# One encoder kernel: values kept in token layout, and the rows of maxima moved by a transfer

## The chip, the core and the metric

The kernel runs on one core of a Trainium2 chip. The core has five engines with instruction streams of their own: TensorE (PE, matmuls), VectorE (DVE), ScalarE (ACT), GpSimd (POOL) and SyncE (SP), which in this kernel issues the transfers (DMAs). They meet at semaphores. The metric is the time of one execution in device microseconds. For the kernel before it is 3714.93 us, the median of three runs (3707.92, 3714.93, 3715.57).

## The reference

Two layers of an encoder run over 1280 tokens of 1024 features: one sequence of 1024 tokens and one of 256, with shared weights. What matters here is the mixer of each layer:

```
h = RMSNorm(x); z = h @ w_in
A: latent attention, 4 heads (keys and values from a low-rank latent, rotary part beside them)
B: dilated windows (128,1), (512,4), (2048,16) joined by their softmax denominators, bias by distance, 4 heads
C: grouped queries, 8 heads on 2 key/value heads, per-head norm of q and k, 2-D rotary
p = softmax(scale * q k^T + bias);  o = p v
x = x + RMSNorm(concat(A, B, C) @ w_out)
x = x + RMSNorm(ConvGatedMLP(RMSNorm(x)))
```

The result is float32 throughout, and the kernel keeps that accuracy on TensorE by splitting each operand into a high and a low part: a product is high x high, low x high and high x low, so three matmuls.

## The kernel before

Each layer runs through phases with a barrier of all engines between them: `latent_projections`, `head_projections`, `attention`, output projection and normalisation, then the gated MLP. The change touches the first three.

**Projections.** Activations lie with features on the partitions and tokens along the row. A projection unit makes 128 features of all 1280 tokens: weights are the stationary operand and tokens the moving one, in blocks of 512, 512 and 256, three matmuls for each of eight chunks of 128 input features (helper `product`, L224 to L226). A unit ends in three banks of PSUM, ACT copies it to a stage buffer in one instruction of 1280 columns (L1034), and SP stores it to a DRAM tensor `heads`, one row per feature (L892). The weights of the next units come in by transfers from SP (L636), ACT rounds them to the high part (L645), and POOL subtracts to get the low part (L650). The phase has twelve units, five of which are roped (norm and rotary) on DVE and POOL; the last three (`VB`, `VC`, `VB+P`) are values. The values of group A come from two units of the latent phase.

**Attention.** Sixteen heads follow each other without a gap (A: 0 to 3, B: 4 to 7, C: 8 to 15). A head is 18 steps, held in the table `STEPS`: query blocks of 512, 512 and 256 columns against tiles of 128 keys. The three blocks begin at steps 0, 4 and 9. On PE, step i is: `scores` (L1288; three matmuls in A, four in B, two in C), then the *side work* that the function `side_work` gives for the step, then `values` of step i-3 (L1300, L1301, L1303). ACT takes the exponential twice (L1412, L1413), DVE subtracts to get the low part of the probabilities, which this text calls `p_low` (L1578). Scores of step i wait for `p_low` of step i-3.

The softmax is shifted by the row's maximum. Maxima of a head come ahead of its steps: 18 matmuls (L1319, in B a bias matmul L1322 behind each) make blocks of q k^T, and DVE reduces them (L1532, L1535, L1542) to columns of the tile `m`, which hold one number per query on 128 partitions. The shift is added inside the scores' matmul, through one extra row of the q operand: partition 96 of `q1` in A, partition 64 of `q2` in B and C. So the columns have to become a row. This is done in three pieces (`ROW_TILES`: 4, 2 and 4 tiles of 128 queries, for the blocks that begin at steps 0, 4 and 9). `turn_row` transposes a strip of 65 columns per tile (L1340) so that the row of interest lands on partition 0 of one PSUM bank with the tiles side by side, and `copy_row` on ACT writes 1 x 512 or 1 x 256 numbers into the q operand's row (L1393). Pieces 0 and 1 are side work of steps 15 and 17 of the head before, piece 2 of step 7 of the head itself. The first scores of a block wait for its piece (`row_copied`).

Nine heads of each layer bring new keys and values (1 to 8 and 12; head 0's are made ready in the phase ahead). Their values lie in DRAM with features on rows, are loaded as 64 x 1280 (`vt`, L1247), turned tile by tile on PE as side work of steps 3 (eight transposes) and 11 (two), both L1330, and split by DVE out of PSUM (L1551, L1553).

**Queues.** The order of each engine is written out by hand; nothing reorders it. SP's order in attention is: q of head h, k of head h, for B two bias lines (`graw`, L1245), values of head h, each behind waits for the buffers that they fill.

## Time and profile before

| | |
|---|---|
| median of three runs | 3714.93 us (3707.92 to 3715.57) |
| the profiled execution's own time | 3715.99 us |
| its span, first to last instruction | 3714.2 us |
| PE busy in the span | 3633.3 us (98%), 18267 matmuls |
| DVE, ACT, POOL busy | 1847.0 (50%), 1552.6 (42%), 1148.6 us (31%) |
| mean granted clock of PE | 0.991 |
| attention, first and second layer (from the span's start) | 325.7 to 799.5 and 2158.0 to 2634.5 us |

How to read it: "busy" is the time in which an engine has an instruction in work. Matmuls overlap, so the duration of one (0.39 us for 512 columns) is longer than what it adds to the engine's time; what it adds is read from the starts of two that follow each other. A matmul row of the profile names out<-in by the program's tiles, `ps` being PSUM. In brackets stands the idle time ahead of an instruction and what ended it.

### The profile page before, as it was taken

Reading aid. Unit: us, or ns where it says so; the run is one execution under the profiler, and the core shown is the slowest. Engines: PE = TensorE matmul, PEld = TensorE weight load, DVE = VectorE, ACT = ScalarE, POOL = GpSimd, SP = SyncE. Lnnn points to the kernel's source line nnn. Section 1 sums busy time; section 2 is a strip of 40 time slices with the busy share of each in tenths; the row PEclk is TensorE's granted clock in tenths of the full one; section 3 lists DMA queues with packets and bytes.
Section 4 is the critical chain, followed back from the end, with each engine's and each line's share of the span. In section 5 each row is a group of like instructions: output and inputs, shape, how many; then the busy total and the mean of one; then the engine's idle time right before and its main releaser. Section 6 shows DMA issues by size and latency. Waiting matters only on the chain. (4 is left out here: it accounts for less than half of the span.)

```text
span 3714.2 us, 49843 instructions
## 1 busy us (share of the span) xinstructions
PE 3633.3 (98%) x18267; PEld 3003.9 (81%) x18267; DVE 1847.0 (50%) x2900; ACT 1552.6 (42%) x2515; POOL 1148.6 (31%) x835
## 2 busy tenths in 40 slices
PE   8999999999999999999999999999999999999998
PEld 7787777778788888888767877777788888888886
DVE  4135868955433333344551367689463333344335
ACT  4334878974222121221442367789542122211213
POOL 1134443443321221221342334434343221221213
PEclk9999999999999999999999999999999999999999
DMA  5342321022111111111324323111221111111113
GB/s 173 124 111 68 75 68 33 22 80 91 46 40 40 40 40 34 40 40 34 113 67 143 97 68 86 47 40 32 71 95 46 40 40 34 40 40 34 35 45 113
DMA packets 205965, 234.00 MB, mean 63 GB/s; under 512 B 15968, under 2 KB 164486, under 8 KB 205767
## 3 DMA queue, kind: packets, MB, share of 16 engines
q1 hardware_dynamic: 205807, 231.93, 21.4%
q8 instruction: 94, 1.54, 0.2%
q14 instruction: 64, 0.52, 0.0%
HBM read 173.86 MB, written 51.48 MB: 61 GB/s over the span
## 5 line engine op out<-in xcount | busy, mean ns | idle before, releaser
L224 PE MATMUL ps<-hh,wh 128*128 128x512 f32 (+1 forms) x2688 | 969.0, 360 | 16.4 <-PEq L218 12.6
L225 PE MATMUL ps<-hl,wh 128*128 128x512 f32 (+1 forms) x2688 | 955.8, 356 | 0.0
L226 PE MATMUL ps<-hh,wl 128*128 128x512 f32 (+1 forms) x2688 | 954.5, 355 | 0.0
L2495 POOL TENSOR_TENSOR wl<-raw,wh 128x1024 fp32r<-128x1024 f32 x126 | 301.7, 2401 | 1269.1 <-ACT wh L2328 1269.1
L224 PEld LDWEIGHTS ps<-hh,wh 128*128 128x128 f32 x2688 | 510.4, 190 | 95.1 <-issue 19.0
L2556 DVE SCALAR_TENSOR_TENSOR cb<-ps,params,cb 128x1023 f32<-128x1023 f32 (+1 forms) x172 | 143.9, 878 | 871.5 <-ACT cb L2337 871.5
L225 PEld LDWEIGHTS ps<-hl,wh 128*128 128x128 f32 x2688 | 510.6, 190 | 76.6 <-issue 5.7
L226 PEld LDWEIGHTS ps<-hh,wl 128*128 128x128 f32 x2688 | 510.1, 190 | 72.1
L1578 DVE TENSOR_TENSOR pl<-ps,ph 128x512 fp32r<-128x512 f32 (+1 forms) x576 | 375.6, 653 | 53.8 <-ACT ps L1413 53.4
L1532 DVE TENSOR_REDUCE mx<-ps 128x1 f32<-128x512 f32 x480 | 330.9, 689 | 142.0 <-PE ps L1322 82.8
L1412 ACT ACTIVATE ph<-ps 128x512 fp32r<-128x512 f32 (+1 forms) x576 | 330.0, 573 | 162.2 <-PE ps L1288 157.1
L1288 PE MATMUL ps<-q,k 97*128 97x512 f32 (+4 forms) x1296 | 384.9, 388 | 8.1 <-PEq L218 6.2
L2337 ACT ACTIVATE cb<-ps,params 128x1280 f32<-128x1280 f32 x86 | 122.3, 1422 | 645.0 <-PE ps L226 635.2
L2587 DVE TENSOR_TENSOR y<-ps,y 128x512 f32<-128x512 f32 (+1 forms) x480 | 279.7, 600 | 179.0 <-PE ps L226 176.4
L224 PE MATMUL ps<-ah,wh 128*128 128x512 f32 (+1 forms) x960 | 341.3, 356 | 0.0
L225 PE MATMUL ps<-al,wh 128*128 128x512 f32 (+1 forms) x960 | 341.3, 356 | 0.0
L226 PE MATMUL ps<-ah,wl 128*128 128x512 f32 (+1 forms) x960 | 339.6, 354 | 0.0
L1413 ACT ACTIVATE ps<-ps 128x512 f32<-128x512 f32 (+1 forms) x576 | 328.6, 571 | 0.0
L2328 ACT ACTIVATE wh<-raw 128x1024 fp32r<-128x1024 f32 x126 | 130.4, 1050 | 431.3 <-PE ps L226 422.3
L1288 PEld LDWEIGHTS ps<-q,k 97*128 97x128 f32 (+2 forms) x1296 | 238.2, 190 | 67.4 <-DVE pl L1578 11.8
L1300 PE MATMUL ps<-ph,vh 128*128 128x512 f32 (+1 forms) x576 | 231.6, 402 | 0.0
L1303 PE MATMUL ps<-pl,vh 128*128 128x512 f32 (+1 forms) x576 | 219.9, 382 | 0.0
(271 smaller groups left out, 5633.7 us busy)
## 6 DMA issues: line engine op xcount, KB each, us to landing
raw<-in_w_up SPq DMA_DIRECT2D x88, 512.0 KB, 3.9
heads<-stage SPq DMA_DIRECT2D x38, 640.0 KB, 3.1
raw<-in_w_down SPq DMA_DIRECT2D x44, 512.0 KB, 3.7
rq<-heads SPq DMA_DIRECT2D x56, 320.0 KB, 4.8
raw<-in_w_in SPq DMA_DIRECT2D x32, 512.0 KB, 4.3
rk<-heads SPq DMA_DIRECT2D x32, 320.0 KB, 4.7
raw<-in_w_out SPq DMA_DIRECT2D x16, 512.0 KB, 4.4
residual<-my SPq DMA_DIRECT2D x32, 256.0 KB, 2.0
```

Of the source, the lines that this page charges most:

```text
L224: pe.matmul(out, wh, xh, start=(k == 0), stop=False)
L225: pe.matmul(out, wh, xl, start=False, stop=False)
L226: last = pe.matmul(out, wl, xh, start=False, stop=(k == len(pairs) - 1))
L1288: mm = pe.matmul(out, a, b, start=(k == 0), stop=(k == len(prods) - 1))
L1300: pe.matmul(out, c.vh[kv(h)][:, kt, :], c.ph[g % RING][:, 0:w], start=first, stop=False)
L1303: pe.matmul(out, c.vh[kv(h)][:, kt, :], c.pl[g % RING][:, 0:w], start=False, stop=last).then_inc(pv_done, 1)
L1412: act.activation(c.ph[g % RING][:, 0:w], scores, ACT.Exp, scale=STEP_SCALE[kind(h)]).then_inc(exp_done, 1)
L1413: act.activation(scores, scores, ACT.Exp, scale=STEP_SCALE[kind(h)]).then_inc(exp_done, 1)
L1532: dve.tensor_reduce(c.mx[:, qt, kb:kb + 1], bank(c, b, w), AX.X, ALU.max).then_inc(max_taken, 1)
L1578: dve.tensor_tensor(c.pl[g % RING][:, 0:w], bank(c, ST + g % 3, w), c.ph[g % RING][:, 0:w].bitcast(F32), ALU.subtract).then_inc(p_low, 1)
L2495: pool.tensor_tensor(c.wl[slot][:], c.raw[parity][:], c.wh[slot][:].bitcast(F32), ALU.subtract).then_inc(w_lo, units)
L2587: dve.tensor_tensor(c.y[:, o, t0:t0 + w], bank(c, DOWN_BANKS[u], w), c.y[:, o, t0:t0 + w], ALU.add).then_inc(down_added, 1)
```

## The change

Values are now computed in token layout. In the head phase the normalised activations are the stationary operand (128 tokens at a time) and the value weights the moving one: ten tiles of 128 tokens, each with eight chunks of three matmuls over 384 columns (all of B's and C's values). In the latent phase five groups of two tiles make A's values, 256 columns each. They are stored to a new DRAM tensor `values`, one row per token. The value weights get buffers of their own, whose low part lies where the buffers of the rotary work lay, so POOL's split of them waits until the fifth unit is roped. In attention, values come in as 128 x 10 x 64 and are split by DVE from that buffer (SBUF), in one piece of 640 columns behind `p_low` of step 9; the transposes on PE are gone.

Each piece of the row of maxima is now one transpose, of 4 or 2 columns of `m` into 4 or 2 partitions of 128. ACT copies those to a small buffer `row_part`, and a transfer from SP moves them into the q operand's row. The first scores of a block wait for the transfer (`row_landed`) instead of the copy. Piece 2 is turned at step 6 in A and head 8, 7 in B, 5 in heads 9 to 15. On SP, pieces 0 and 1 of head h-2 stand ahead of the q loads of head h, and piece 2 behind the k loads and ahead of the bias lines.

```diff
+def value_columns(c, col):
+    return c.s_v[:, col:col + 64].rearrange("(t p) n -> p t n", p=P)
+def split_head_values(dve, c, slot, n):
+    dve.tensor_copy(c.vh[slot][:, :, 0:64], c.vt[:]).then_inc(c.v_hi, 1)
+    dve.wait_ge(c.v_hi, n + 1)
+    dve.tensor_tensor(c.vl[slot][:, :, 0:64], c.vt[:], c.vh[slot][:, :, 0:64].bitcast(F32), ALU.subtract).then_inc(c.v_lo, 1)
...
-    UNITS = 12
+    UNITS = 9
+    LOADS = 12
...
+                pe.wait_ge(w_lo, LOADS - 2)
+                for t in range(NT):
+                    pe.wait_ge(evacuated, UNITS - 1 if t < 3 else UNITS if t < 6 else UNITS + t - 5)
+                    ts = slice(t * P, t * P + P)
+                    product(pe, bank(c, VALUE_BANKS[t % 6], V_COLS),
+                            [(c.hh[:, k, ts], c.hl[:, k, ts], c.wv_hi[:, k, :], c.wv_lo[k // 5][:, k % 5, :]) for k in range(KC)],
+                            lambda k: side(KC * t + k)).then_inc(w_used, 1)
...
+                            pool.wait_ge(w_hi, UNITS + u - 1)
+                            pool.wait_ge(roped, len(ROPED))
+                            pool.tensor_tensor(c.wv_lo[0][:, :, cols], raw[:, 0:5, :], c.wv_hi[:, 0:5, cols].bitcast(F32), ALU.subtract)
...
+    OUT_SPLITS = ((HEADS - 2, 11), (HEADS - 2, 16), (HEADS - 1, 7), (HEADS - 1, 12))
...
+    def third_row(h):
+        return 19 - max_lead(h)
...
-        if i in (3, 11) and h >= 0 and new_kv(h + 1):
-            work.append(("values", h + 1, (i - 3) // 8))
-        if i == 7 and 0 < h < HEADS:
+        if 0 < h < HEADS and i == third_row(h):
             work.append(("row", h, 2))
...
+                def move_row(h, r):
+                    t0, t1 = ROW_TILES[r]
+                    sp.wait_ge(row_copied, 3 * h + r + 1)
+                    row = c.q1[h % 3][96:97, :] if kind(h) == "A" else c.q2[h % 3][64:65, :]
+                    sp.dma_start(row[:, t0 * P:t1 * P].bitcast(F32).rearrange("a (k p) -> a k p", p=P),
+                                 c.row_part[r][0:t1 - t0, :].bitcast(F32)).then_inc(row_landed[r], 16)
...
-                    if first:
-                        pe.wait_ge(row_copied, 3 * h + block + 1)
+                    if first and h == 0:
+                        pe.wait_ge(row_copied, block + 1)
+                    elif first:
+                        pe.wait_ge(row_landed[block], 16 * h)
...
-                    for k, qt in enumerate(range(*ROW_TILES[r])):
-                        m0 = max_column(qt)
-                        mm = pe.transpose(bank(c, b, P, slice(0, ROW_WINDOW), off=k * P), c.m[:, m0:m0 + ROW_WINDOW], c.ident[:])
-                    mm.then_inc(row_turned, 1)
+                    m0 = max_column(ROW_TILES[r][0])
+                    pe.transpose(bank(c, b, P, slice(0, row_tiles(r))), c.m[:, m0:m0 + row_tiles(r)], c.ident[:]).then_inc(row_turned, 1)
...
-                    t0, t1 = (x * P for x in ROW_TILES[r])
-                    row = c.q1[h % 3][96:97, t0:t1] if kind(h) == "A" else c.q2[h % 3][64:65, t0:t1]
-                    act.activation(row, bank(c, b, t1 - t0, slice(0, 1)), ACT.Copy).then_inc(row_copied, 1)
+                    if h >= 2:
+                        act.wait_ge(row_landed[r], 16 * (h - 1))
+                    rows = slice(0, row_tiles(r))
+                    act.activation(c.row_part[r][rows, :], bank(c, b, P, rows), ACT.Copy).then_inc(row_copied, 1)
...
+                    if i == 9 and new_kv(h + 1):
+                        split_values(h + 1)
```

Where the work stands on the engines, before and after, is shown at three places. (The numbers behind a name tell buffers of one name apart.)

On PE, head 1, step 3: between the side matmul of a maximum and the values of an earlier step stand the eight transposes of head 2's values.

```order
L1319 MATMUL ps<-k_1_114,q_1_108 128x512
L1330 MATMUL ps<-ident,vt 128x64 x8
L1300 MATMUL ps<-ph_131,vh_123 128x512
L1301 MATMUL ps<-ph_131,vl_125 66x512
L1303 MATMUL ps<-pl_135,vh_123 128x512
```

In the changed kernel the values (now L1396) follow the maximum (now L1415) at once.

```order
L1415 MATMUL ps<-k_1_114,q_1_108 128x512
L1396 MATMUL ps<-ph_132,vh_123 128x512
L1397 MATMUL ps<-ph_132,vl_125 66x512
L1399 MATMUL ps<-pl_136,vh_123 128x512
L1384 MATMUL ps<-q_1_108,k_1_114 128x256
```

On PE, head 5 (kind B), steps 7 to 9: piece 2 of the row is turned, and two groups of values and the scores of step 8 later the first scores that need it begin.

```order
L1340 MATMUL ps<-ident,m 65x128 x4
L1300 MATMUL ps<-ph_131,vh_123 128x256
L1301 MATMUL ps<-ph_131,vl_125 66x256
L1303 MATMUL ps<-pl_135,vh_123 128x256
L1288 MATMUL ps<-q_2_116,k_1_114 128x512
L1288 MATMUL ps<-q_2_119,k_1_115 128x512
L1288 MATMUL ps<-gh_189,flip_r 128x512
L1288 MATMUL ps<-gl_191,flip_r 128x512
L1319 MATMUL ps<-k_0_120,q_0_117 128x512
L1322 MATMUL ps<-gh_188,ident_r 128x512
L1300 MATMUL ps<-ph_132,vh_123 128x512
L1301 MATMUL ps<-ph_132,vl_125 66x512
```

In the changed kernel one transpose (L1427) stands in the place of four, with the same work behind it.

```order
L1427 MATMUL ps<-ident,m 4x128
L1396 MATMUL ps<-ph_132,vh_123 128x256
L1397 MATMUL ps<-ph_132,vl_125 66x256
L1399 MATMUL ps<-pl_136,vh_123 128x256
L1384 MATMUL ps<-q_2_116,k_1_114 128x512
L1384 MATMUL ps<-q_2_119,k_1_115 128x512
L1384 MATMUL ps<-gh_196,flip_r 128x512
L1384 MATMUL ps<-gl_198,flip_r 128x512
L1415 MATMUL ps<-k_0_120,q_0_117 128x512
L1418 MATMUL ps<-gh_195,ident_r 128x512
L1396 MATMUL ps<-ph_133,vh_123 128x512
L1397 MATMUL ps<-ph_133,vl_125 66x512
```

On SP in attention, the transfers for head 4: its q and k (`rq`, `rk`), its bias lines and its values.

```order
L1224 DMA rq<-heads 64x1280 x2
L1238 DMA rk<-heads 64x1280 x2
L1245 DMA graw_186<-distance_lines 128x960
L1245 DMA graw_187<-distance_lines 128x960
L1247 DMA vt<-heads 64x1280
```

In the changed kernel head 2's three pieces of the row (L1284) stand among them, two ahead of the q loads and the third between the k loads and the bias lines.

```order
L1284 DMA q_2_116<-row_part_126 1x4x128
L1284 DMA q_2_116<-row_part_140 1x2x128
L1302 DMA rq<-heads 64x1280 x2
L1318 DMA rk<-heads 64x1280 x2
L1284 DMA q_2_116<-row_part_141 1x4x128
L1327 DMA graw_193<-distance_lines 128x960
L1327 DMA graw_194<-distance_lines 128x960
L1329 DMA vt<-values 128x10x64
```

## Rows read from the trace of the kernel before

**Rows 1.** Busy time in the two attention stretches: their sum, then each engine.
```profile
sum 950.30, PE 947.02 PEld 736.14 DVE 772.90 ACT 782.95 POOL 430.80; mean PE 473.51 PEld 368.07 DVE 386.45 ACT 391.48 POOL 215.40
```

**Rows 2.** Timeline of PE, head 1 step 3 (start us, duration us, engine, line, instruction).
```profile
359.76 0.40 PE L1319 MATMUL ps<-k,q 96*128 96x512 f32 x1
360.09 0.71 PE L1330 MATMUL ps<-ident,vt 64*128 64x64 f32 x8
...
361.06 0.40 PE L1301 MATMUL ps<-ph,vl 128*66 128x512 f32 x1
```

**Rows 3.** Timeline of PE, head 0 step 11, the pair of transposes.
```profile
343.58 0.33 PE L1330 MATMUL ps<-ident,vt 64*128 64x64 f32 x2
...
344.19 0.39 PE L1301 MATMUL ps<-ph,vl 128*66 128x512 f32 x1
```

**Rows 4.** Timeline of PE, end of a C head into the next.
```profile
745.91 0.39 PE L1319 MATMUL ps<-k,q 128*128 128x512 f32 x1
746.14 0.60 PE L1340 MATMUL ps<-ident,m 128*65 128x128 f32 x4
...
746.81 0.39 PE L1301 MATMUL ps<-ph,vl 128*66 128x512 f32 x1
...
747.97 0.28 PE L1300 MATMUL ps<-ph,vh 128*128 128x256 f32 x1
748.09 0.28 PE L1301 MATMUL ps<-ph,vl 128*66 128x256 f32 x1
...
749.03 0.38 PE L1340 MATMUL ps<-ident,m 128*65 128x128 f32 x2
...
749.48 0.40 PE L1301 MATMUL ps<-ph,vl 128*66 128x512 f32 x1
...
749.95 0.63 PE L1288 MATMUL ps<-q,k 128*128 128x512 f32 x2
```

**Rows 5.** Timeline of ACT in the same stretch.
```profile
747.48 0.59 ACT L1393 ACTIVATE q<-ps 1x512 fp32r<-1x512 f32 x1
```

**Rows 6.** Timeline of ACT, head 5 step 7.
```profile
503.84 0.58 ACT L1393 ACTIVATE q<-ps 1x512 fp32r<-1x512 f32 x1
```

**Rows 7.** Timeline of PE, head 5 step 9, first scores.
```profile
505.85 0.63 PE L1288 MATMUL ps<-q,k 128*128 128x512 f32 x2
```

**Rows 8.** DMA issues: out<-in, queue, count, KB each, median us to landing.
```profile
raw<-in_w_in SPq DMA_DIRECT2D x32, 512.0 KB, 4.3
residual<-my SPq DMA_DIRECT2D x32, 256.0 KB, 2.0
...
rot<-stage SPq DMA_DIRECT2D x80, 80.0 KB, 2.6
```

**Rows 9.** Timeline of PE, the first matmuls of attention.
```profile
325.70 2.00 PE L1288 MATMUL ps<-q,k 97*128 97x512 f32 x5 [3.21 <-PEq L218]
```

**Rows 10.** Timeline of DVE, head 1 steps 9 to 11.
```profile
373.03 0.68 DVE L1578 TENSOR_TENSOR pl<-ps,ph 128x512 fp32r<-128x512 f32 x1
...
374.66 0.28 DVE L1551 CAST vh<-ps 128x128 fp32r<-128x128 f32 x1
...
375.18 0.68 DVE L1578 TENSOR_TENSOR pl<-ps,ph 128x512 fp32r<-128x512 f32 x1
```

**Rows 11.** Timeline of PE, head 1 step 13, its scores.
```profile
376.63 0.52 PE L1288 MATMUL ps<-q,k 97*128 97x256 f32 x3
```

**Rows 12.** Timeline of DVE in the head phase, the fifth roped unit.
```profile
260.89 1.49 DVE L1101 TENSOR_TENSOR rot<-rot,st 128x1280 f32<-128x1280 f32 x1
263.43 2.91 DVE L1104 TENSOR_TENSOR stage<-rot,pr 128x1280 f32<-128x1280 f32 x1 [1.05 <-ACT pr L1000]
```

**Rows 13.** Timeline of POOL in the same stretch.
```profile
262.59 2.40 POOL L650 TENSOR_TENSOR wl<-raw,wh 128x1024 fp32r<-128x1024 f32 x1 [8.19 <-ACT wh L645]
```

**Rows 14.** Timeline of ACT in the head phase, units 7 and 8.
```profile
261.47 1.05 ACT L645 ACTIVATE wh<-raw 128x1024 fp32r<-128x1024 f32 x1
...
274.54 1.24 ACT L1034 ACTIVATE stage<-ps 128x1280 f32<-128x1280 f32 x1 [11.21 <-PE ps L226]
```

More of the change, by code:

```diff
@@ L171, in place_buffers @@
     c.vl = [take(f"vl{i}", [P, NT, VL_COLS], F32R) for i in range(2)]
+    vl_end = at[0]
+    c.row_part = [take("row_part0", [P, P], F32R)]
     at[0] = max(at[0], projections_end)
@@ L698, in _ @@
                 sp.dma_start(c.s_z[QAR:QAR + P, :], c.stage[1][:]).then_inc(stored[1], 16)
-                for j in range(2, 8):
+                for j in range(2, 6):
                     sp.wait_ge(evacuated, 3 + j)
@@ L755, in _ @@
                             aux(9 + b, [(c.perm_a[:], c.stage[1][:, t0:t0 + w])], slice(0, P), w)
+                for g in range(5):
+                    pe.wait_ge(evacuated, 7 if g < 3 else 8)
+                    for i in range(2):
+                        ts = slice(256 * g + P * i, 256 * g + P * i + P)
+                        last = product(pe, bank(c, VALUE_BANKS[g], 256, off=256 * i),
+                                       [(c.lath[:, 2, ts], c.latl[:, 2, ts], c.kv_hi[:, 256:512], c.kv_lo[:, 256:512])])
+                    last.then_inc(unit_done, 1)
             @block.scalar
@@ L791, in _ @@
                 act.activation(c.lath[:, 2, :], c.lat[2][:], ACT.Copy).then_inc(lat_hi, 1)
-                for j in range(1, 8):
+                for j in range(1, 6):
                     m = 3 + j
@@ L801, in _ @@
                         act.activation(c.wh[i][:], c.raw[i][:], ACT.Copy).then_inc(head_hi, 1)
+                for g in range(5):
+                    act.wait_ge(unit_done, 6 + g)
+                    act.activation(value_stage(g), bank(c, VALUE_BANKS[g]), ACT.Copy).then_inc(evacuated, 1)
             @block.gpsimd
@@ L889, in store, with store_values @@
                         sp.wait_ge(evacuated, n + 1)
-                    done = stored[n % 3] if n < UNITS - 3 else c.heads_stored
-                    sp.dma_start(c.s_z[rows[n]:rows[n] + P, :], c.stage[n % 3][:]).then_inc(done, 16)
+                    sp.dma_start(c.s_z[rows[n]:rows[n] + P, :], c.stage[n % 3][:]).then_inc(stored[n % 3], 16)
+                def store_values(tiles):
+                    for t in tiles:
+                        sp.wait_ge(evacuated, UNITS + t + 1)
+                        sp.dma_start(c.s_v[t * P:t * P + P, VB:VB + V_COLS], value_stage(t)).then_inc(c.heads_stored, 16)
                 def turn(n):
@@ L901, in turn @@
                         sp.dma_start(c.rot[n % 2][g:g + 16, :], c.stage[n % 3][from_row:from_row + 16, :]).then_inc(turned[n % 2], 16)
[L903 removed]
+                for n in range(2, LOADS):
                     if n - 4 in ROPED:
@@ L912, in _ @@
                 sp.dma_start(c.rq[64:96, :], c.s_z[QAR + 32:QAR + 64, :]).then_inc(c.q_raw, 16)
-                for n in range(UNITS - 4, UNITS - 2):
-                    store(n)
+                store(UNITS - 1)
                 sp.wait_ge(c.k_lo, 3)
@@ L1017, in _ @@
                         roots(n - 1, (0, 1))
-                    if n == TURN_ROWS:
-                        for r in range(3):
-                            first_row(r)
                     act.wait_ge(w_used, n + 1)
@@ L1107, in _ @@
                     first_maximum(j)
-                for part in range(2):
-                    first_values(part)
+                dve.wait_ge(head0, 16 * 5)
+                split_head_values(dve, c, 0, 0)
         end_phase(nc, raw_arrived + [w_hi, w_lo, w_used, tables, evacuated, squared, unit_sum, sum_read, turn_read,
@@ L1204, in side_read @@
                 return max_taken, NM * h + j + 1
-            if what == "values":
-                return v_lo, 2 * (kv_count(h) - 1) + j + 1
             return row_copied, 3 * h + j + 1
@@ L1215, in _ @@
                         continue
+                    if h >= 3:
+                        for r in range(2):
+                            move_row(h - 2, r)
                     sp.wait_ge(q_hi, 3 * h)
@@ L1253, in _ @@
                     sp.dma_start(c.raw[n % 2][:], out_unit(c, L, n)).then_inc(weights[n % 2], 16)
+                for r in range(3):
+                    move_row(HEADS - 2, r)
+                sp.wait_ge(scored, NS * 14)
+                for n in range(2):
+                    load_out_weights(n)
+                for r in range(2):
+                    move_row(HEADS - 1, r)
+                for n in range(2, 4):
+                    load_out_weights(n)
+                move_row(HEADS - 1, 2)
+                for n in range(4, OUT_EARLY + 2):
+                    load_out_weights(n)
                 for i in range(2):
@@ L1323, in max_scores @@
                     mm.then_inc(max_scored, 1)
-                def turn_values(h, part, b):
-                    if h >= 1:
-                        pe.wait_ge(v_raw, 16 * (kv_count(h) - 1))
-                    for t in (range(8) if part == 0 else range(8, 10)):
-                        mm = pe.transpose(bank(c, b, 64, off=(t % 8) * 64), c.vt[0:64, t * P:t * P + P], c.ident[0:64, 0:64])
-                    mm.then_inc(v_turned, 1)
                 def turn_row(h, r, b):
@@ L1352, in _ @@
                             max_scores(h, j, side_bank[item])
-                        elif what == "values":
-                            turn_values(h, j, side_bank[item])
                         else:
@@ L1570, in _ @@
                             take_max(head, j, side_bank[what, head, j])
-                        elif what == "values":
-                            split_values(head, j, side_bank[what, head, j])
                     if 0 <= g < G_TOTAL:
@@ L2737, in encoder @@
     c.s_z = nc.dram_tensor("heads", (Z_ROWS, T), F32, kind="Internal").ap()
+    c.s_v = nc.dram_tensor("values", (T, Z_COLS), F32, kind="Internal").ap()
     c.s_line = nc.dram_tensor("distance_lines", (H_B, N_DIST), F32, kind="Internal").ap()
```

163 lines of the change are left out of this document (93 added, 70 removed).

## The prediction

> **What bounds the kernel now.** I read the busy times of the whole span first: TensorE is busy 98% of it, every other engine half or less. Then the two attention stretches by windows: PE 947.0 of 950.3 us [rows 1], so 3.3 us of idle time lies in them, and whatever leaves PE's order there shortens the kernel by what it adds to that order, unless a new wait takes its place. Last I read the timelines around each kind of instruction that the change touches, and always the starts: a matmul of 512 columns adds 0.235 us to PE's time (two lie between 749.48 and 749.95), one of 256 columns 0.12 (747.97 to 748.09) [rows 4].
>
> **What goes.** Transposes of values. Head 1's eight: the maximum ahead starts at 359.76, the second values matmul behind at 361.06 [rows 2]. Without the transposes these two would lie 2 x 0.235 apart, so the eight cost 1.30 - 0.47 = 0.83 us. From the first transpose to that matmul it is 0.97 [rows 2], with two transposes 0.61 (343.58 to 344.19) [rows 3]: six fewer save 0.36, so two cost 0.47. Nine heads in two layers: 18 x (0.83 + 0.47) = 23.4 us. Head 0's values are turned in the same way in the head phase, also on PE: 2 x 1.30 = 2.6.
>
> Transposes of the rows. Four take 0.90 (745.91 to 746.81) minus 0.47 = 0.43; two take 0.22 less (746.14 to 746.81 against 749.03 to 749.48: 0.67 and 0.45) [rows 4], so 0.21. One is then about 0.11. Fifteen heads, two layers: 60 of four and 30 of two become 90 single ones: 25.8 + 6.3 - 9.9 = 22.2. If a single transpose cost as much as a pair, it would be 13.2.
>
> Evacuation at the end of two phases. The last copy of 1280 columns takes 1.24 (274.54) [rows 14], 512 take 0.59 [rows 5], so a column adds 0.85 ns, 384 take 0.48, a latent group's 512 take 0.59. PE waits for the store and the barrier behind that copy, 3.21 us ahead of attention [rows 9]. Two layers: 2 x (0.76 + 0.65) = 2.8.
>
> **What is added on PE.** The value products have the columns of before (per layer 240 x 384 = 3 units x 24 x 1280 in the head phase, 30 x 256 = 2 x 3 x 1280 in the latent one), but 36 more matmuls. A cut adds 2 x 0.12 - 0.235, at most 0.01 [rows 4]: 72 x 0.013 = 0.9 us at most, which I take.
>
> **The value weights' wait.** POOL may split them only when the fifth roped unit is done. DVE's last step of it starts at 263.43 and takes 2.91 beside POOL's split of a unit's weights, which ends at 264.99 [rows 12, 13]. In the changed kernel that split is what waits, so the step may take the 1.49 of its neighbour [rows 12] and end at 264.92, or 266.34 as now. Then for the third set: POOL's split of the first set frees its buffer (2.40) [rows 13], the load lands 4.3 later [rows 8], ACT rounds it (1.05) [rows 14], POOL splits it (2.40): 10.2 us with nothing for the hand-overs, 275.1 or 276.5. PE is done with unit 8 shortly ahead of 274.54 [rows 14], say 274.4: it waits 0.7 to 2.1 us. I take the middle with a little for hand-overs, 1.6, twice: 3.2. The nearest cover is the matmuls of that unit itself; a load that lands at twice 4.3 would make it 6 each.
>
> **Rows that come by a transfer.** This is the largest unknown: no row shows a transfer of 2 KB between partitions of SBUF. The nearest rows are the 128 x 512 store (2.0 us to landing) and the stage-to-rot moves inside SBUF, which go in trains of eight (2.6) [rows 8]; a load of 512 KB takes 4.3 [rows 8]. I take 1.95, with 1.7 and 3.5 as ends. To it comes ACT's copy (0.59 - 384 x 0.85 ns = 0.26) [rows 5, 14] and some 0.03 to the issue, a guess. The time that is there is read from before as the start of ACT's copy to the first scores of the block, less the PE time that the transposes gave up between them. Piece 0 in C: 747.48 to 749.95 = 2.47 [rows 4, 5], less 0.32 for its own turn (ACT's copy follows exponentials of scores ahead of the turn, so it stays where it is while the first scores come sooner) and 0.1 for piece 1's: 2.05. Piece 2 in B: 503.84 to 505.85 = 2.01 [rows 6, 7], less 0.32 = 1.69; head 7's follows with three matmuls less and has about 1.2. By the same reading piece 0 of A has 2.7, piece 2 of A (now one step earlier) 2.6, of head 8 2.4, of C (two steps earlier) 3.5, and piece 1 over 5 anywhere. Needed are 0.29 + 1.95 = 2.24: C's piece 0 waits 0.19 (heads 9 to 15, two layers: 14 x 0.19 = 2.7), B's piece 2 0.55 (6 x = 3.3), head 7's 1.04 (2 x = 2.1): 8.1 us. At 1.7 it is 3.4, at 2.6 some 26, at 3.5 some 67, since then A's pieces wait too. On SP piece 2 stands behind k loads, which wait for POOL's split of the keys before, work of steps 0 to 2 of that head, so they are out ahead of the turn. Behind the pieces stand the bias lines, which the next head but one uses, and the q loads, which may now leave only after step 17 of head h-3, but which POOL needs from step 9 of head h-2. So I cost the queue at nothing; if a load's wait ran past the turn, piece 2 would land later by as much.
>
> **The split by DVE.** It is one block of two instructions on 640 columns, where before 512 columns were split at step 3 and 128 at step 11. A two-operand instruction between SBUF tiles of 1280 columns takes 1.49 [rows 12], so I take 0.8 for each half, 1.6 in all. In A: `p_low` of step 9 starts at 373.03, gives DVE free at 373.65, the split runs to 375.25, the maximum (0.61 as the step between starts) to 375.86, `p_low` of step 10 to 376.54; scores of step 13 start at 376.63 [rows 10, 11]. It just fits, because the two small instructions that go (374.66 to 375.18, 0.52) [rows 10] stood in the same gap. The next `p_low` is then some 0.3 late: 8 x 0.3. In B a step has more matmuls and it fits. Head 11's steps are the shortest (two matmuls of scores): about 1 us late, twice. Sum 2.4 + 2 = 4.4. It is 0 if the halves take half of that, and 18 x (1.49 + 0.1) at most if each waits out another engine as the row of 2.91 did: 29.
>
> On that row: DVE's step is held 1.4 us while POOL reads SBUF [rows 12, 13]. The Trainium skill ("SBUF — State Buffer", Who interferes with whom) says why: DVE and GpSimd share one pair of ports by an exclusive lock, and a DVE instruction with two SBUF inputs, or a copy in a two-port mode, fully blocks against GpSimd. The trace agrees (2.91 against 1.49). It speaks against the change, since values were split out of PSUM before and are now split from SBUF; it is the second rival below. The skill's "VectorE: DVE Perf Modes" (Mode 2×_2P) would make the rounding copy twice as fast between SBUF buffers. No row here shows such a copy; by that rule the sum would be some 3 us lower.
>
> **Sum.** Gone: 23.4 + 2.6 + 22.2 + 2.8 = 51.0. Added: 0.9 + 3.2 + 8.1 + 4.4 = 16.6. 3715.99 - 34.4 = 3681.6 for an execution like the profiled one; the median lies 1.1 below that one's own time, so 3680.5, and I write 3681.
>
> **Rivals.** (1) The new waits are covered: the landing is 1.7 or less and DVE and the weights make nobody wait. Then 47 to 50 go: 3665 to 3668, 3666. For it: a piece is 2 KB, and the 2.0 is that of 256 KB. Against it: B's piece 2 has 1.69 us, which asks for a landing of 1.4.
> (2) DVE's split is held by POOL. POOL splits q of the head after next at its steps 9, 11 and 13, around DVE's step 9. If each split takes 3.0 instead of 1.6 (the 1.4 of the held row on top), the excess by the same chain of starts is 1.7 in A (0.9 in head 3), 0.4 to 1.2 in B, 2.3 in head 11, together 21 instead of 4.4: 3697. Against it: POOL is busy 430.8 of 950.3 us [rows 1], so a split meets it less than half the time.
> (3) The pieces land late, which makes it slower. Place: the first scores of blocks 0 and 2, 60 of 90 pieces. From a landing of 2.6 on, a further 0.9 costs 41 us, so 46 per us; the gain of 34.4 on top of 8.1 is used up at 2.6 + (42.5 - 26) / 46 = 2.96 us. At 3.5 the time is 3681 + 59 = 3740. For it: 512-byte pieces and a destination of one partition, and loads that share the queue. Against it: the moves inside SBUF take 2.6 though they leave eight at a time [rows 8].
> (4) A single transpose has a fixed cost and takes what a pair does: 9 us less gain, 3690. The step from four to two (0.22) speaks for proportion.
>
> **Chances and range.** The forecast 0.58; (1) 0.14; (2) 0.12; (3) 0.10; (4) 0.06. The likeliest case alone, with landings of 1.7 to 2.2 and DVE's term between 0 and 9, spans 3672 to 3692. The range holds (1), (2), (4) and landings to 2.6 (3681 + 18 = 3699); with DVE held and a landing of 2.4 (18 instead of 8.1) it is 3707, where it ends. Its low end stands 4 under (1): PE's waits for DVE's split out of PSUM, behind the values transposes, go too, and the sum leaves them out. About 0.2% (7.4 us) is what a measurement of this kernel can tell from no change. Faster by more: 0.58 + 0.14 + 0.06 and most of (2), 0.87. Within it: 0.05, the part of (3) near 2.9 and worst sums of (2). Slower: 0.08.
>
> **What would show it.** PE's row turns are single matmuls that push the next start by 0.11; PE's busy time in the two attention stretches falls by some 45 us. Waits of scores that begin a block show who is late: on a DMA from `row_part` in C's block 0 and B's block 2, by 0.2 and 0.55, or not. The transfers' median landing decides between (1), the forecast and (3). The rows of the split on DVE show 0.8 and 0.8, or one of 1.5 and more with POOL beside it. In the head phase PE stands idle 1 to 2 us ahead of the first value product. The forecast is wrong if the landing is over 2.2, if the scores of steps 13 and 14 wait for DVE by more than 0.5 in A, or if PE waits where nothing of this is.

## The result and the profile after

The changed kernel takes 3677.25 us (median of four runs, 3675.38 to 3678.59); the kernel before, beside it, 3715.25 (3707.92 to 3717.63). The ratio is 0.9901 with an interval of 0.9889 to 0.9912, so 37 us less, where 34 were forecast (3681). The span of the profiled execution falls from 3714.2 to 3676.4.

The first lines of the page after the change: the span, then busy time, share of the span and number of instructions of each engine.

```profile
span 3676.4 us, 49277 instructions
...
PE 3588.7 (98%) x17929; PEld 2974.7 (81%) x17929; DVE 1833.9 (50%) x2860; ACT 1525.4 (41%) x2535; POOL 1151.8 (31%) x841
```

TensorE's share is still 98%, so the kernel became shorter by what left PE's order, less what turned into waiting. To see how much that is, both traces are cut at the same events: from attention's first scores to its last. First the kernel before, then the changed one (window, its length, busy us of each engine, granted clock as a share of full speed, share of the DMA engines, GB/s).

```profile
325.70:796.65 470.95, 469.26 (x2227) 364.94 (x2228) 384.60 (x670) 389.25 (x758) 214.66 (x234) 1.00 0.21 51
2158.04:2631.55 473.51, 471.96 (x2227) 366.88 (x2228) 384.62 (x670) 389.32 (x758) 214.65 (x234) 0.99 0.20 51
sum 944.46, PE 941.22 PEld 731.82 DVE 769.22 ACT 778.57 POOL 429.30; mean PE 470.61 PEld 365.91 DVE 384.61 ACT 389.28 POOL 214.65
```

```profile
326.56:779.84 453.28, 447.92 (x2032) 344.36 (x2033) 379.76 (x652) 374.39 (x758) 215.74 (x234) 1.00 0.21 53
2140.44:2595.30 454.86, 449.13 (x2033) 345.60 (x2034) 380.96 (x652) 374.56 (x758) 215.87 (x234) 1.00 0.21 53
sum 908.14, PE 897.06 PEld 689.96 DVE 760.72 ACT 748.95 POOL 431.61; mean PE 448.53 PEld 344.98 DVE 380.36 ACT 374.48 POOL 215.81
```

PE is busy 44.2 us less (45 was forecast), the stretches are 36.3 shorter; PE's idle time in them rises from 3.2 to 11.1. Some 2.6 us of the 36.3 are not the change but the clock that PE was granted in the execution before (the account of the prediction ends with it). The remaining 1.5 us of the span went in the other phases. What PE waits for in the first layer's stretch now (us in total, times, longest):

```profile
PE ps L1384 <- DVE pl L1656: 2.9, 7, 0.8
PE ps L1384 <- PEq L235: 2.2, 1, 2.2
PE ps L1415 <- ACT gh L1471: 1.1, 1, 1.1
PE ps L1384 <- DMA q<-row_part: 0.6, 1, 0.6
```

The second row is the barrier ahead of attention (its start stands for [rows 9]). The other three are for DVE's split (before, 0.9 us in four waits for `p_low` stood here) and for a row piece, which the forecast had, and for ACT's `gh`, which it had not. This view counts only idle time, and a wait comes out larger when it is read from the starts of the matmuls; the amounts below are from starts.

The row piece of head 4, block 2. (Head 5, which [rows 6] and [rows 7] show before, waits by the same 0.29.) PE, with the single transpose at 458.90:

```profile
458.67 0.39 PE L1418 MATMUL ps<-gh,ident_r 128*128 128x512 f32 x1
458.90 0.27 PE L1427 MATMUL ps<-ident,m 128*4 128x128 f32 x1
458.92 0.36 PE L1396 MATMUL ps<-ph,vh 128*128 128x256 f32 x1
459.13 0.28 PE L1397 MATMUL ps<-ph,vl 128*66 128x256 f32 x1
...
461.21 0.39 PE L1399 MATMUL ps<-pl,vh 128*128 128x512 f32 x1
461.74 0.47 PE L1384 MATMUL ps<-q,k 128*128 128x512 f32 x1
```

ACT's copy, and SP's issue of the transfer with the first bias line behind it:

```profile
459.65 0.25 ACT L1478 ACTIVATE row_part<-ps 4x128 fp32r<-4x128 f32 x1
```

```profile
459.92 0.65 SPq L1284 DMA_DIRECT2D q<-row_part  x1
460.62 0.44 SPq L1327 DMA_DIRECT2D graw<-distance_lines  x1
```

From 458.67 to 459.13 are 0.46; less 0.235 and 0.12 for the two matmuls, the transpose adds 0.11. From issue to the scores that wait are 461.74 - 459.92 = 1.82 us. The scores would have begun at 461.21 + 0.235 = 461.45, so the wait is 0.29. The packet records of the trace divide the 1.82: the piece's four packets lie between 461.21 and 461.30, so 1.29 us pass from the issue to the first packet, 0.09 in the packets and 0.44 from the last one to the scores. Of all 90 pieces the first packet begins 1.22 to 1.34 us behind the issue.

DVE's split, head 0 in the second layer, with POOL and PE beside it (`CAST vh<-vt` and the subtraction behind it stand where [rows 10] has `CAST vh<-ps`):

```profile
2156.18 0.68 DVE L1656 TENSOR_TENSOR pl<-ps,ph 128x512 fp32r<-128x512 f32 x1
2156.78 0.93 DVE L619 CAST vh<-vt 128x640 fp32r<-128x640 f32 x1
2157.74 1.79 DVE L621 TENSOR_TENSOR vl<-vt,vh 128x640 fp32r<-128x640 f32 x1
2159.46 0.68 DVE L1617 TENSOR_REDUCE mx<-ps 128x1 f32<-128x512 f32 x1
```

```profile
2156.75 0.61 POOL L1527 CAST q<-rq 96x512 fp32r<-96x512 f32 x1
2157.44 1.41 POOL L1534 TENSOR_TENSOR q<-rq,q 96x512 fp32r<-96x512 f32 x1
```

```profile
2160.79 0.39 PE L1384 MATMUL ps<-q,k 97*128 97x256 f32 x1 [1.30 <-DVE pl L1656]
```

This is the dearest of the 18 splits in attention: 2.7 us, and the scores of step 13 wait. Over all 20 of the kernel the second half takes 825 ns at least and 826 in the median; the smallest, the median and the largest stand here in ns:

```profile
L621 DVE TENSOR_TENSOR vl<-vt,vh x20: 825/826/1795, 304.2 to 2491.9; 128x640 fp32r<-128x640 f32 x20
```

### The profile page after: what moved, and what is told of

It is laid out like the page before. It is cut to its first block and busy times, and to the rows that moved or that the text cites. A ratio compares the mean times of both kernels' runs of the same rounds, so it can differ in the third digit from the quotient of the medians.

```text
span 3676.4 us, 49277 instructions
## 1 busy us (share of the span) xinstructions
PE 3588.7 (98%) x17929; PEld 2974.7 (81%) x17929; DVE 1833.9 (50%) x2860; ACT 1525.4 (41%) x2535; POOL 1151.8 (31%) x841
## 3 DMA queue, kind: packets, MB, share of 16 engines
q8 instruction: 91, 1.49, 0.2%
## 5 line engine op out<-in xcount | busy, mean ns | idle before, releaser
L241 PE MATMUL ps<-hh,wh 128*128 128x512 f32 (+1 forms) x2544 | 917.0, 360 | 18.2 <-PEq L235 14.3
L242 PE MATMUL ps<-hl,wh 128*128 128x512 f32 (+1 forms) x2544 | 904.1, 355 | 0.0
L243 PE MATMUL ps<-hh,wl 128*128 128x512 f32 (+1 forms) x2544 | 903.1, 355 | 0.0
L241 PEld LDWEIGHTS ps<-hh,wh 128*128 128x128 f32 x2544 | 483.3, 190 | 92.7 <-issue 20.8
L242 PEld LDWEIGHTS ps<-hl,wh 128*128 128x128 f32 x2544 | 483.4, 190 | 72.4 <-issue 5.7
L243 PEld LDWEIGHTS ps<-hh,wl 128*128 128x128 f32 x2544 | 482.7, 190 | 68.1
L1396 PE MATMUL ps<-ph,vh 128*128 128x512 f32 (+1 forms) x576 | 226.8, 394 | 0.0
```

Source lines behind the costliest of these rows:

```text
L241: pe.matmul(out, wh, xh, start=(k == 0), stop=False)
L242: pe.matmul(out, wh, xl, start=False, stop=False)
L243: last = pe.matmul(out, wl, xh, start=False, stop=(k == len(pairs) - 1))
L1396: pe.matmul(out, c.vh[kv(h)][:, kt, :], c.ph[g % RING][:, 0:w], start=first, stop=False)
```

## The experiments

Each was timed in five rounds beside the kernel before. The intervals are some 5 to 6 us to either side, so a term of 3 us is read from the traces, and the times only have to agree.

**One part alone.** `values_only` takes the values in token layout and leaves four transposes per row; `rows_only` moves the rows by a transfer and leaves the values. Of `side_work`, against the changed kernel, the first:

```diff
-        if 0 < h < HEADS and i == third_row(h):
+        if i == 7 and 0 < h < HEADS:
```

and the second:

```diff
+        if i in (3, 11) and h >= 0 and new_kv(h + 1):
+            work.append(("values", h + 1, (i - 3) // 8))
```

> The kernel before with the token-layout values alone: products, stores, loads and DVE's split as changed, the rows of maxima as before (four or two transposes, ACT's copy, piece 2 at step 7). By the prediction's terms: 23.4 + 2.6 + 2.8 less 0.9, 3.2 and 4.4, so 20.3 us faster than before (ratio 0.9945). Rival: DVE's split from SBUF and the new value weights give back most of what the transposes gave, then under 8 us faster (over 0.998). If the two parts are independent, this gain and that of the rows alone add up to the 38 us of the whole; if both end at the same engine in some heads (ACT in head 3, DVE in C), their sum is larger by 3 us or more.

> The kernel before with the moved rows alone (one transpose per piece, ACT's copy of 4 partitions, transfer, piece 2 at step 6, 7 or 5), values as before. By the prediction's terms 22.2 less 8.1, so 14 us faster (0.996); by the waits that the changed kernel's trace shows on row_part (3.2 instead of 8.1) 19 us (0.995). Rival: the transfers land in time only because the values' transposes are gone, and here SP's or DMA's queue makes them late: then over 8 us of waits on row_part and a gain under 14.

Measured: values alone 0.9945 (0.9931 to 0.9958), 20 us less; rows alone 0.9948 (0.9934 to 0.9962), 19 less. Together 40, the whole change 37 with intervals of about 5 on each: within these the parts add. In the traces they do so in most heads. Head 1, from its first scores to the next head's, takes 30.33 before, 29.23 with values alone, 29.63 with rows alone, 28.50 with both (1.10 + 0.70 against 1.83). Head 7 takes 35.56, 34.25, 35.66 and 34.33: there the rows alone cost 0.10, since piece 2 comes late. Head 3 gets only 0.28 from values alone (33.93 to 33.65), and its trace says why: the wait for ACT stands there already without the rows.

```profile
421.98 0.47 PE L1377 MATMUL ps<-k,q 128*128 128x512 f32 x1 [1.24 <-ACT gh L1435]
```

**The landing.** `b_row6` turns piece 2 of B heads a step earlier; `bias_first` lets the bias lines go ahead of it.

```diff
-        return 19 - max_lead(h)
+        return 18 - max_lead(h) if 4 <= h < 8 else 19 - max_lead(h)
```

```diff
-                    if h >= 3:
-                        move_row(h - 2, 2)
                     if kind(h) == "B":
...
                             sp.dma_start(c.graw[i][:], src).then_inc(table_raw, 16)
+                    if h >= 3:
+                        move_row(h - 2, 2)
                     sp.wait_ge(v_lo, n)
```

> The changed kernel with piece 2 of the B heads turned at step 6 instead of 7 (as A has it). The changed kernel waits 0.29 us for it in heads 4 to 6 and 0.72 in head 7, in both layers 3.2 us, and with one step (2 us) more all of that goes, unless the last maximum of a B head (step 5) isn't reduced when PE comes to the turn: by DVE's rows that takes some 0.9 us of the 2.1 of a step, so PE shouldn't wait. 3 us less than the changed kernel, some 40 under before. Rival: the piece is late because SP or the queue is, not because its turn is; then the wait on row_part stays at 0.29 and 0.72.

> The changed kernel with piece 2 of head h-2 behind the bias lines of head h on SP instead of ahead of them (heads 4 to 7). By the prediction the place costs nothing unless a load's wait runs past the turn: the lines of heads 5 to 7 wait for POOL's low part of the table before (issued at steps 7.5, 6.8 and 6.8 of heads 3 to 5 in the kernel before), so piece 2 of head 3 lands about 1 to 1.5 us later and its scores at step 9 wait by some 1 us; heads 2, 4 and 5 wait by 0 to 0.7 more: 1.5 to 5 us slower than the changed kernel over both layers. Rival: the lines ahead cost nothing, or bring a gain, since the table of head 4 comes sooner.

`b_row6` came as expected: 0.988 (0.9865 to 0.9895), 3673.45; all waits for rows are gone and no other came. Heads 4 to 7 are 4.0 us shorter over both layers. `bias_first` missed by far: 0.9943 (0.993 to 0.9957), 3694.47, 17 us over the changed kernel. SP and PE in head 2:

```profile
389.08 1.06 SPq L1325 DMA_DIRECT2D graw<-distance_lines  x2
391.49 0.66 SPq L1284 DMA_DIRECT2D q<-row_part  x1
```

```profile
396.66 0.70 PE L1384 MATMUL ps<-q,k 97*128 97x512 f32 x2 [2.54 <-DMA q<-row_part]
```

The issue is not late here (ACT's copy, at 391.21, sets it; in head 3 alone it comes 1.3 us behind the copy), but from issue to scores it takes 5.17 us, in heads 3 to 5 3.81, 3.03 and 2.94. The rows' waits sum to 17.9 us over both layers instead of 3.2.

**Is it the queue?** I took it that a piece waits behind the lines in SP's own queue. `row2_act` gives it another: ACT issues piece 2 of heads 2 to 5 right behind its copy.

```diff
-                    if h >= 3:
+                    if h >= 3 and kind(h) != "B":
                         move_row(h - 2, 2)
...
                     act.activation(c.row_part[r][rows, :], bank(c, b, P, rows), ACT.Copy).then_inc(row_copied, 1)
+                    if r == 2 and 2 <= h <= 5:
+                        act.wait_ge(row_copied, 3 * h + r + 1)
...
+                        act.dma_start(row[:, 4 * P:8 * P].bitcast(F32).rearrange("a (k p) -> a k p", p=P),
+                                      c.row_part[2][0:4, :].bitcast(F32)).then_inc(row_landed[2], 16)
```

> The changed kernel with piece 2 of heads 2 to 5 issued by ACT right behind its copy, from ACT's own queue, so that SP issues the bias lines at once as in the kernel before, ahead of the piece in time. With the lines ahead on SP's queue the piece of head 2 took 5.17 us from its issue to the scores, against 1.81 where nothing stands ahead. If a transfer waits for those issued earlier on its own queue, the piece on ACT's queue lands as fast as ever: waits of at most 0.3 us in heads 4 and 5 and none in 2 and 3, the time of the changed kernel or 1 us more for ACT's issues. Rival: the lines keep the 16 engines busy whoever issues; then the scores of heads 2 and 3 wait over 1.5 us as they did with the lines first, and the time is some 10 us over the changed kernel.

Measured: 0.9938 (0.9924 to 0.9951), 3689.97, 13 over the changed kernel: the theory of the queue falls. Head 3: ACT's issue, SP's lines, the scores, and the stretch between (the last two numbers but one are PE's granted clock and the DMA engines' share):

```profile
426.81 0.61 ACTq L1482 DMA_DIRECT2D q<-row_part  x1
```

```profile
427.01 0.80 SPq L1327 DMA_DIRECT2D graw<-distance_lines  x2
```

```profile
430.86 0.47 PE L1384 MATMUL ps<-q,k 97*128 97x512 f32 x1 [1.18 <-DMA q<-row_part]
```

```profile
426.81:430.86 4.05, 2.87 (x14) 2.03 (x13) 2.65 (x5) 2.12 (x4) 3.53 (x5) 1.00 0.50 185
```

The piece is issued 0.20 us ahead of the lines, on another queue, and takes 4.05 us all the same, with the 16 DMA engines half busy. In the changed kernel's head 4 the same stretch is 1.82 long and the engines are idle:

```profile
459.92:461.74 1.82, 1.68 (x9) 1.02 (x7) 1.25 (x3) 1.09 (x2) 1.52 (x3) 1.00 0.00 1
```

So what delays a small transfer is a large one in work beside it, whichever queue it came by. The packet records show where: in head 3 the lines' packets run from 428.34 on, and the piece's own four, 0.2 us long together, come only at 430.02, 3.21 behind the issue. Nor is ACT's queue slow by itself. In heads 4 and 5, where the lines' packets begin 0.9 to 1.0 us ahead of the issue in both kernels, the piece's first packet comes 2.0 to 2.3 us behind the issue on SP's queue (`bias_first`) and 2.1 to 2.2 on ACT's. What the piece waits for ahead of its first packet, no run shows. What the order on SP buys is 0.7 us of start ahead of the lines (459.92 against 460.62), and that was enough. The Trainium skill ("DMA: Bandwidth & Descriptors", Issuing engines are not separate DMA queues) says that the queues of the issuing engines share the same 16 DMA engines; the 4.05 agrees with it.

**The split by DVE.** `split12` does it at step 12; `poolq12` leaves it and moves POOL's split of q from steps 9, 11, 13 to 12, 14, 16.

```diff
-                    if i == 9 and new_kv(h + 1):
+                    if i == 12 and new_kv(h + 1):
```

```diff
-                    if i in (9, 11, 13) and h + 2 < HEADS:
+                    if i in (12, 14, 16) and h + 2 < HEADS:
...
```

> The changed kernel with DVE's split of the values behind p_low of step 12 instead of 9. Step 13 is a block of 256 columns, so its p_low is short and its scores come with more slack. If the lost time is the split's place in DVE's chain, PE's waits for p_low at steps 13 and 14 in heads 0, 1, 2 and 11 (5.3 us over both layers) fall to under 1.5, and the kernel is some 4 us faster than the changed one: about 41 under before. Rival: the split holds PE wherever it stands, then the waits move to steps 16 and 17 with the same sum and the time stays.

> The changed kernel with POOL's split of q at steps 12, 14 and 16 instead of 9, 11 and 13; DVE's split stays at step 9. If POOL's reads of SBUF hold DVE's split, all 18 splits in attention take 0.48 and 0.83 us (in the changed kernel up to 0.94 and 1.79 in heads 0, 2 and 3), PE's waits at steps 13 and 14 of heads 0 and 2 fall to the 0.13 of head 1 (together some 2.5 us less), and head 11's 1.0 stays. Rival: the long ones have another cause (the load of the next values, ACT), then they stay.

`split12`: 0.9891 (0.9876 to 0.9906), 3672.14. Every split takes 0.48 and 0.83, and the waits of the scores of steps 13 and 14 are gone; in their place maxima wait by 0.20 in head 1 and 0.50 in head 11, where a row's turn waits by 0.36 too.

```profile
L621 DVE TENSOR_TENSOR vl<-vt,vh x20: 825/826/828, 302.2 to 2486.2; 128x640 fp32r<-128x640 f32 x20
```

`poolq12`: 0.9895 (0.988 to 0.991), 3673.74. In head 2 POOL no longer stands beside, the split is short and the wait falls from 0.50 to 0.13; head 11 keeps 0.84 and 0.91 of its 1.00 and 0.98: its steps are too short for 1.3 us, with POOL beside or not.

```profile
396.65 0.48 DVE L619 CAST vh<-vt 128x640 fp32r<-128x640 f32 x1
397.17 0.83 DVE L621 TENSOR_TENSOR vl<-vt,vh 128x640 fp32r<-128x640 f32 x1
```

Head 0 was not helped: its split still meets POOL (0.91 and 1.79 in the first layer), since POOL's instructions there follow their loads and not the steps. Where POOL is beside it the split is long, where it is not it is short, in three kernels: that settles what holds it. The Trainium skill ("SBUF — State Buffer", Who interferes with whom) says that the two engines share a pair of SBUF ports by a lock, and that the one that comes second waits for the whole instruction of the first; the long rows agree.

**ACT's table.** In head 3 ACT rounds B's bias table at steps 3 and 4. `table_early` does that at steps 13 and 15 of head 2.

```diff
+                    if i in (13, 15) and h == 2:
+                        split_table(4, (i - 13) // 2)
-                    if i in (3, 4) and kind(h + 1) == "B":
+                    if i in (3, 4) and h >= 4 and kind(h + 1) == "B":
```

> The changed kernel with ACT's rounding of head 4's bias table (two of 0.99 us) moved from steps 3 and 4 of head 3 to steps 13 and 15 of head 2. The changed kernel waits 1.28 us at step 6 of head 3 for the second of them, in each layer. If ACT's own order in the first steps of head 3 is the cause (six roundings of k, two of the table, and the exponentials), that wait goes and so does part of head 3's 0.67 at step 4: 2.6 to 4 us less than the changed kernel. Rival: the bias lines come late, since they stand behind piece 2 on SP; then ACT waits for them in head 2 and PE loses there what it gains in head 3.

0.9889 (0.9874 to 0.9905), 3674.22. The wait for `gh` is gone from both layers; a wait of 0.67 at step 4 of head 3 stays, and one layer has a new one of 0.8 in head 3's first steps.

**The stores of the latent values.** `stores3` sends the five stores of 256 tokens as three.

```diff
-                for g in range(5):
+                for g, n in ((0, 2), (2, 2), (4, 1)):
...
```

> The changed kernel with A's values stored from the latent phase in three transfers (512, 512 and 256 tokens) instead of five. PE stands idle 3.5 and 3.7 us behind that phase in the changed kernel, 2.7 and 3.1 before, though ACT's last copy is shorter. If SP's issues are what the barrier waits for (0.77 us each, the last three from 135.00 to 137.30), two fewer take 1 to 1.5 us off each gap: 2 to 3 us in all. Rival: the landing of the last store or its rows of 1 KB set it; then the gaps stay.

0.9886 (0.987 to 0.9901), 3672.76. PE's gap between the two projection phases, by starts, falls from 3.76 to 2.64 and from 4.00 to 3.07. SP and PE in the changed kernel:

```profile
133.34 1.62 SPq L740 DMA_DIRECT2D values<-pln  x2
135.00 2.30 SPq L740 DMA_DIRECT2D values<-lat  x3
```

```profile
138.81 0.76 PE L241 MATMUL ps<-hh,wh 128*128 128x512 f32 x1 [3.48 <-PEq L235]
```

and in `stores3`:

```profile
135.58 1.33 SPq L740 DMA_DIRECT2D values<-lat  x2
```

```profile
138.00 0.47 PE L241 MATMUL ps<-hh,wh 128*128 128x512 f32 x1 [2.36 <-PEq L235]
```

By the medians it gave 4.5 us, more than the 2.05 of the two gaps. In these two executions the clock behind the gap differs as well. The 5 us behind it, changed kernel and then `stores3`:

```profile
138.81:143.81 5.00, 5.00 (x12) 3.93 (x13) 0.24 (x1) 1.24 (x1) 0.00 (x0) 0.50 0.63 161
```

```profile
138.00:143.00 5.00, 5.00 (x22) 4.14 (x23) 0.24 (x1) 1.25 (x1) 0.00 (x0) 1.00 0.58 176
```

Behind 3.48 us of idleness PE is granted 0.50 (1.2 GHz) and does 12 matmuls in 5 us; behind 2.36 it is granted 1.00 (2.4 GHz) and does 22. But the shorter gap is not shown to be the reason. `table_early` has the five stores and a gap of 3.47, `all_four` (below) has the three and, in the second layer, a gap of 2.74; the 5 us behind them:

```profile
139.01:144.01 5.00, 5.00 (x22) 4.14 (x23) 0.24 (x1) 1.24 (x1) 0.00 (x0) 1.00 0.63 161
```

```profile
1941.74:1946.74 5.00, 5.00 (x12) 3.94 (x13) 0.24 (x1) 1.24 (x1) 0.00 (x0) 0.50 0.41 122
```

So the clock behind this barrier differs from execution to execution at the same gap, and what the three stores are shown to give is the 2.05 us.

**All together.** `all_four` is `split12`, `b_row6`, `table_early` and `stores3` in one; `changed_again` is the changed kernel once more, beside it.

```diff
+        return 18 - max_lead(h) if 4 <= h < 8 else 19 - max_lead(h)
...
+                    if i in (13, 15) and h == 2:
...
+                    if i == 12 and new_kv(h + 1):
...
+                for g, n in ((0, 2), (2, 2), (4, 1)):
```

> The changed kernel once more, beside the one with all four edits, so that both are set against the same runs of before. 38 us under before, as measured (0.990).

> The changed kernel with four edits together: DVE's split behind step 12, piece 2 of B at step 6, head 4's table rounded in head 2, three stores for A's values. Each alone brought 5.1, 3.8, 3.0 and 4.5 us under the changed kernel's median. If they act at different places they add up: 16 us under the changed kernel, 54 under before (ratio 0.9855). Rival: they share an engine, DVE at steps 12 to 16 or ACT in head 2, and give back part of it: then the sum stays under 11.

`changed_again`: 0.9901 (0.9885 to 0.9918), 3676.58. `all_four`: 0.9875 (0.9859 to 0.9891), 3666.39, the fastest of all, but 10 under the changed kernel, not 16. That looks as if the four repairs got in each other's way, and at one place they do a little: with the table's rounding at step 15 of head 2, ACT's copy of head 3's piece 0 stands behind it, and the first scores of head 3 wait by 0.88 and 0.55 (by starts) for the row.

```profile
401.12 1.00 ACT L1471 ACTIVATE gh<-graw 128x960 fp32r<-128x960 f32 x1
402.01 0.25 ACT L1478 ACTIVATE row_part<-ps 4x128 fp32r<-4x128 f32 x1
```

```profile
404.41 0.93 PE L1384 MATMUL ps<-q,k 97*128 97x512 f32 x3 [0.71 <-DMA q<-row_part]
```

But `table_early` alone has 0.8 of this 1.4 already. In the traces the repairs nearly add: by the lengths of the heads in attention, and by PE's gap for the stores, they give 4.4 (`split12`), 4.0 (`b_row6`), 2.0 (`table_early`) and 2.05 (`stores3`) one by one, 12.5 in sum, and 12.3 at the same places of `all_four`. The 16 was the sum of four differences of medians, each with some 5 us of doubt.

## Why the prediction was right

The mechanism was right: PE was the bound, what left its order came back as time, and the waits took a fifth of it. That the sum came within 3 us of the measured gain is in part luck: the landings and the weights cost some 7 us less than forecast, and ACT's rounding, the gap between latents and heads and DVE's split took at least 6 more. Two of the forecast's own signs of being wrong came true: the scores of step 13 wait for DVE by 1.45 us in head 0 of the second layer, more than 0.5 in A, and PE waits for ACT in head 3, where nothing of the forecast is. By steps:

- **Values' turns**, 23.4 forecast. Before, they held 25.6 by starts. Of the 2.2 more, 1.4 are a wait for one of DVE's maxima ahead of head 3's eight transposes (0.7 in each layer), which the forecast left out, and 0.9 belong to head 0 in the second layer, where the granted clock was lower.
- **Rows' turns**, 22.2 forecast; 33.4 became 9.7, so 23.7. A single one adds 0.11: rival 4 falls.
- **Rows' landings**, 8.1 forecast, 3.2 measured: six waits of 0.29 and two of 0.72. The term was mis-sized by the landing: 0.25 for the copy and 1.82 to the scores, where 0.29 + 1.95 was taken. From its issue to the scores, C's piece 0 has 1.84 to 1.88 us in heads 9, 11, 13 and 15 and 2.03 or more in the others, so the 14 waits of 0.19 (2.7) did not come. The forecast's 1.95 leaned on the 2.0 of a 256 KB store [rows 8]; rivals 1 and 3 both fall, rival 3 by 1.1 us of landing (it needed 2.96). How narrow that is, `bias_first` shows: landings of 3 to 5 us are what this kernel gets when the lines are ahead.
- **DVE's split**, 4.4 forecast, 5.05 measured at the scores that wait, made otherwise (with what comes late behind them it is 7.2, see below). Alone it takes 1.31, not 1.6, and would cost less; beside POOL it takes up to 2.7. The waits of steps 13 and 14: head 0 0.38 and 1.45 (first and second layer), head 1 0.13 twice, head 2 0.50 and 0.48, head 11 1.00 and 0.98. So rival 2 is true in part: held in heads 0, 2 and 3 and by 0.15 in head 11, free in the others. The Trainium skill's rule for the rounding copy ("VectorE: DVE Perf Modes", Mode 2×_2P) held: 0.48 for a copy of 640 columns against 0.83 for two inputs.
- **The value weights' wait**, 3.2 forecast, 0.8 measured (0.5 and 0.3). The forecast took the middle of 0.7 to 2.1; the low end was right. Since POOL's split waits, DVE's step has no POOL beside it and takes 1.49, the time of its neighbours, instead of the 2.91 of [rows 12]:

```profile
264.66 1.49 DVE L1166 TENSOR_TENSOR stage<-rot,pr 128x1280 f32<-128x1280 f32 x1
```

- **The phases' ends**, a gain of 2.8 forecast. Ahead of attention the gap fell by 1.6 over two layers, as forecast (1.5). Between latents and heads this step failed: 1.3 less was forecast, and the gap rose by 1.35 (2.99 to 3.76, 3.42 to 4.00). The forecast looked at the copy that ends the phase and not at SP behind it, which issues five stores; the last three take 2.30, 0.77 each, and end at 137.30, and the barrier is behind them. `stores3` shows it.
- **Not in the sum**: ACT's rounding in head 3, 1.28 and 1.30. Before, its second half ended at 426.83, and the maximum that is summed with it started at 426.98; now they are at 422.59 and 422.73:

```profile
425.84 0.99 ACT L1387 ACTIVATE gh<-graw 128x960 fp32r<-128x960 f32 x1
```

```profile
426.98 0.48 PE L1319 MATMUL ps<-k,q 128*128 128x512 f32 x1
```

```profile
421.60 0.99 ACT L1471 ACTIVATE gh<-graw 128x960 fp32r<-128x960 f32 x1
```

```profile
422.73 0.48 PE L1415 MATMUL ps<-k,q 128*128 128x512 f32 x1 [1.13 <-ACT gh L1471]
```

  PE started 0.15 behind ACT then and 0.14 now: there was no room, though the row of before shows no idle time. `table_early` shows that the rounding was the cause.

In attention 25.6 + 23.7 went and 3.2 + 5.05 + 2.6 came back: 38.4, where the windows give 36.3. This balance does not close, for four amounts are missing from it:

- Behind a wait the next matmul of the scores comes late as well, by 0.10 to 0.11 where DVE was awaited and 0.07 to 0.08 where the row was, and step 14 of heads 0 and 2 waits by 0.11 to 0.12, as head 1's does. With these DVE's split costs 7.2 us and the rows' landings 4.0, as much as `b_row6` gave back.
- Some short waits for DVE of the kernel before went too (0.9 us in the first layer's stretch).
- C's heads without new keys became shorter by 0.6 each where 0.77 left PE's order. DVE is busy there some 23.3 us of 24.3, which may be the new bound; no run tested that, and it stays open.
- The clock. Head 0 has the same instructions in both layers, but before it took 28.48 us in the first, with 0.94 granted, and 31.05 in the second:

```profile
2158.04:2189.09 31.05, 31.05 (x128) 23.65 (x129) 20.22 (x36) 21.34 (x42) 16.19 (x20) 0.84 0.27 67
```

  In the changed kernel head 0 has 1.00 and 0.94, so some 2.6 of the 36.3 us are the clock of that one execution. The times, medians of several executions, do not rest on it.

## What to carry to other kernels

Where one engine is busy 98% of the time, an edit that takes instructions from its order is worth the differences of starts, summed; then go through every engine that has to be ready sooner, also those that the change does not touch, as each has only the room that the removed work gave it. A small transfer on the path has to leave well ahead of the large ones in time, not only in its queue (0.7 us ahead was enough here, 0.20 was not). Count the issue time of every store that a barrier waits for. Before a difference of a few us between two traces is given to a cause, compare the granted clock behind the barriers.

## What the runs showed of the hardware

- A transfer of 2 KB from one place of SBUF to another takes 1.81 to 1.84 us from issue to the matmul that waits, in each case of the changed kernel that waited; 1.28 to 1.30 of it pass ahead of the first packet. Beside loads of 480 KB it takes 2.8 to 5.3, by its own queue or another's (`bias_first`, `row2_act`).
- What a hold costs DVE is no factor: it takes its own time, less 0.12 to 0.15 us, from where POOL's instruction ends. That is so in all 12 halves of the changed kernel's 20 splits that were held. POOL's at 2157.44 ends at 2158.85; 0.83 more is 2159.68, and DVE's ended at 2159.53. Its copy: 2157.36 + 0.48 = 2157.84 against 2157.71. The step of before [rows 12, 13]: 264.99 + 1.49 = 266.48 against 266.34.
- PE's granted clock behind the barrier between latents and heads was 0.50 for 5 us behind gaps of 3.48 (changed kernel, first layer) and 2.74 (`all_four`, second layer), and 1.00 behind 3.47 (`table_early`, first layer) and 2.36 (`stores3`, first layer): the length of the gap alone does not tell which it will be. From its first matmul to that of attention the head phase took 184.97 us in `table_early` and 187.75 in the changed kernel, so the lower level cost 2.8.
